# Where the four slots of split weights lie in on-chip memory, in an fp32 three-block network

## What is computed

```python
x = layer_norm(DN_ALPHA * x + y, mix_ln_g[layer], mix_ln_b[layer])
x = layer_norm(DN_ALPHA * x + swiglu(x, ffn_w_gate[layer], ffn_w_up[layer], ffn_w_down[layer]), ...)
...
ff = jnp.square(jax.nn.relu(h2 @ w_ff1 + b_ff1)) @ w_ff2 + b_ff2
```

## Times and profile before

| What | Value |
|---|---|
| median of 3 runs | 3581.85 us (3581.0 to 3584.57) |
| the profiled execution, device time | 3582.25 us |
| its span from first to last instruction | 3580.5 us |
| TensorE busy | 3502.4 us, 98% of the span, 16054 matmuls |
| VectorE busy | 1783.9 us, 50% |
| ScalarE busy | 1235.5 us, 35% |
| GpSimd busy | 527.4 us, 15% |
| mean granted TensorE clock | 0.986 of full speed |

### The profile page before, as it was taken

The page is one execution under the profiler, slowest core; times in us unless marked ns, Lnnn a source line. Parts: engine busy times, 40 slices in busy tenths (PEclk is TensorE's granted clock), DMA queues, the critical chain, the costliest instruction groups (busy, mean ns, idle before and its releaser), DMA issues. The chain is left out here.

```text
span 3580.5 us, 41711 instructions
## 1 busy us (share of the span) xinstructions
PE 3502.4 (98%) x16054; PEld 2830.2 (79%) x16054; DVE 1783.9 (50%) x2319; ACT 1235.5 (35%) x1795; POOL 527.4 (15%) x302
## 2 busy tenths in 40 slices
PE   9999999999999999999999999999999899999998
PEld 7768888888887777767888888888876778888886
DVE  7986423233256666567423233564567674323235
ACT  4444410111144444455321112355454442212133
POOL 0007100000052000013100000353223530000004
PEclk9999999999999999999999999999999999999999
DMA  3102213122122111112213123322231222111112
GB/s 106 38 33 89 95 59 112 47 78 87 47 82 83 48 42 47 41 58 78 89 59 106 52 83 110 95 89 94 97 98 44 77 89 94 47 47 53 47 59 100
DMA packets 77474, 259.12 MB, mean 72 GB/s; under 512 B 10288, under 2 KB 11696, under 8 KB 77360
## 3 DMA queue, kind: packets, MB, share of 16 engines
q1 hardware_dynamic: 77360, 257.59, 22.4%
HBM read 244.45 MB, written 4.72 MB: 70 GB/s over the span
## 5 line engine op out<-in xcount | busy, mean ns | idle before, releaser
L208 PE MATMUL ps<-xh,whi 128*128 128x512 f32 x2712 | 943.0, 394 | 14.8 <-POOL xl L500 8.2
L208 PE MATMUL ps<-xh,wlo 128*128 128x512 f32 x2712 | 935.3, 391 | 0.0
L208 PE MATMUL ps<-xl,whi 128*128 128x512 f32 x2712 | 935.2, 391 | 0.0
L191 DVE TENSOR_TENSOR wlo<-stage,whi 128x1024 fp32r<-128x1024 f32 (+1 forms) x361 | 507.2, 1405 | 475.7 <-ACT whi L184 474.5
L184 ACT ACTIVATE whi<-stage 128x1024 fp32r<-128x1024 f32 (+1 forms) x361 | 378.0, 1047 | 978.4 <-PE ps L208 952.8
L208 PEld LDWEIGHTS ps<-xh,whi 128*128 128x128 f32 x2712 | 511.8, 189 | 130.8 <-DVE wlo L191 8.5
L208 PEld LDWEIGHTS ps<-xh,wlo 128*128 128x128 f32 x2712 | 511.8, 189 | 107.8
L208 PEld LDWEIGHTS ps<-xl,whi 128*128 128x128 f32 x2712 | 511.9, 189 | 105.4
L208 PE MATMUL ps<-hh,whi 128*128 128x512 f32 x1216 | 415.4, 391 | 4.0 <-DVE wlo L191 1.9
L208 PE MATMUL ps<-hh,wlo 128*128 128x512 f32 x1216 | 414.0, 390 | 0.0
L208 PE MATMUL ps<-hl,whi 128*128 128x512 f32 x1216 | 413.8, 390 | 0.0
(11 more groups left out here) (453 smaller groups left out, 4008.7 us busy)
## 6 DMA issues: line engine op xcount, KB each, us to landing
stage<-in_w_ff SPq DMA_DIRECT2D x88, 512.0 KB, 3.5
stage<-in_w_gate SPq DMA_DIRECT2D x59, 512.0 KB, 3.4
stage<-in_w_up SPq DMA_DIRECT2D x59, 512.0 KB, 3.4
stage<-in_w_in SPq DMA_DIRECT2D x50, 512.0 KB, 3.4
ada<-in_w_ada SPq DMA_DIRECT2D x48, 512.0 KB, 3.5
stage<-in_w_qkv SPq DMA_DIRECT2D x43, 512.0 KB, 3.4
stage<-in_w_down SPq DMA_DIRECT2D x48, 448.0 KB, 3.3
stage<-in_w_out SPq DMA_DIRECT2D x24, 512.0 KB, 3.4
```

The costliest lines, as they stand in the source:

```text
L191: dve.tensor_tensor(wlo[slot][:, n], stage[slot][:, n], whi[slot][:, n].bitcast(F32), ALU.subtract).then_inc(w_split, 1)
L208: done = pe.matmul(acc[:, h * HALF:(h + 1) * HALF], wt[slot][:, w], xt[:, b, h * HALF:(h + 1) * HALF], start=b == 0 and wt is whi and xt i ...
```

## The change

Eleven small tiles and `cols` and `ident` are allocated in another order, so that some lie ahead of each slot. The slots are no longer one block: `whi0` starts 192 bytes past a multiple of 512, `whi1` 256, `wlo0` 384 and `wlo1` 448. Each slot is as large as before. `x`, `xh`, `xl`, `stage` and the region with `hh` and `hl` stay at the addresses that they had. `ident` starts 448 bytes past a multiple of 512 and not at one. The instructions of each engine, their order, their shapes and their waits are the same.

```diff
     stage = [sb(f"stage{k}", [P, D]) for k in range(2)]
-    WHI_AT = [nc.sbuf_base + 4 * D * k for k in range(2)]
-    whi = [sb(f"whi{k}", [P, D], F32R) for k in range(2)]
-    WLO_AT = [nc.sbuf_base + 4 * D * k for k in range(2)]
-    wlo = [sb(f"wlo{k}", [P, D], F32R) for k in range(2)]
-    cols = sb("cols", [P, NCOLS])
-    ident = sb("ident", [P, P])
+    stats = sb("stats", [P, 2, 2, 6])
     one = sb("one", [P, 1])
     share = sb("share", [P, 2])
-    stats = sb("stats", [P, 2, 2, 6])
     eps = sb("eps", [P, 1])
+    WHI_AT = [-(-nc.sbuf_base // 32) * 32]
+    whi = [sb("whi0", [P, D], F32R)]
     credit = sb("credit", [P, 9])
-    ps = [ctx.enter_context(nc.psum_tensor(f"ps{k}", [P, S], F32)) for k in range(4)]
+    WHI_AT += [-(-nc.sbuf_base // 32) * 32]
+    whi += [sb("whi1", [P, D], F32R)]
     gb2 = sb("gb2", [P, DB])
     ada_sum = sb("ada_sum", [P, 2])
     lam_t = sb("lam_t", [P, 8])
     mx = sb("mx", [P, 2, 2])
+    WLO_AT = [-(-nc.sbuf_base // 32) * 32]
+    wlo = [sb("wlo0", [P, D], F32R)]
     nb = sb("nb", [P, 2, 2])
     den = sb("den", [P, 2, 2])
+    WLO_AT += [-(-nc.sbuf_base // 32) * 32]
+    wlo += [sb("wlo1", [P, D], F32R)]
+    cols = sb("cols", [P, NCOLS])
+    ident = sb("ident", [P, P])
+    ps = [ctx.enter_context(nc.psum_tensor(f"ps{k}", [P, S], F32)) for k in range(4)]
     rden = sb("rden", [P, 2, 2])
```

## The result

The changed kernel takes 3625.76 us (median of 4 runs, 3624.03 to 3634.66), the kernel before 3581.43 beside it (4 runs, 3580.15 to 3584.57): a ratio of 1.0127 with a 95% interval of 1.011 to 1.0145. The change costs 44 us. The forecast was 81 us less; the time lies inside the range, on the side of the slower rival.

What follows compares the result with a forecast made beforehand. The prediction took TensorE's stream of 512-column matmuls at a 226.7 ns pitch as the bound. Half of 12.7 ns, 6.35 ns x 12,792 = 81 us, came off 3582 to give 3501 us; range 3420 to 3642.

Steps and rivals of the forecast that it cites:

- the slower rival: L208 stretches: with `whi` and `wlo` 192 bytes apart the pitch stays at 231.7 ns; 59 us added, 3641 us; chance 0.28.
- What bounds the kernel: TensorE's stream of 512-column matmuls, 12,792 at a pitch of 226.7 ns, 2,900 us, four fifths of the time.
- I forecast that they do [meet less at a distance]: 512-column matmuls: weight loads and moving operand meet less when their starts differ modulo 512; half of 12.7 ns goes, 81 us.
- The price that I put at -6.35 ns: Expected pitch change per 512-column matmul at L208 and L1349; over 12,792 matmuls, 81 us saved.
- The likeliest case: Fewer meetings in the 512-column stream: 3420 to 3575 us, likeliest 3501; chance 0.44.
- Reads of the next weights in the way of reads of the moving operand: Mechanism claimed for the 12.7 ns by which the 512-column pitch of 226.7 exceeds 214 ns.
- the 12.7 ns: Part of the steady 226.7 ns pitch of 512-column matmuls over 214 ns; all of it gone would save 162 us.
- the bound: Upper limit for L208: the pitch stays for good at its unsettled 231.7 ns, adding 59 us.
- The sign that the two slots would have pitches of their own: Profile after, at L208: if slots count singly, units in slot 0 and slot 1 have two different pitches.
- the settling after a break: Trace before: six pitches after a break average 231.7 ns, the next five 226; taken as two streams meeting in a pattern.
- the rival of no change: 512-column stream: the extra 12.7 ns are paid whatever the addresses, so time stays 3582 us; chance 0.28.
- the 260-column matmuls: At L3050, 120.0 ns each, 11.3 over 108.7; expected to gain or lose about as much each as 512-column ones.

Runs made afterwards that it cites:

- The fourth kernel of set 1: Against the kernel before: both `whi` at multiples of 512 and both `wlo` 192 bytes past one, by moving four small tiles between them; 3621.35 us.

## Why the prediction came out as it did

**What bounds the kernel: right.** The stream of 512-column matmuls sets the time, the pitch is the whole question, and the four measures that I wanted unchanged (counts, order, load length, ScalarE and VectorE) are unchanged. `ident` and `cols` cost nothing that shows: all slots at 256 with both moved came to 3580.87.

**"I forecast that they do [meet less at a distance]": the step that failed.** It rested on two streams that start in the same piece being "the worst pair". The reverse is so: of all settled values 226.67 at distance 0 is the lowest, and none of the 18 kernels of the experiments has a pitch below it in its long piece. The price that I put at -6.35 ns is +4.35. The likeliest case had the wrong sign. It also counted the 1,008 matmuls of L1349 at the same price. In their pieces of six they stand at 231.3 ns before and 232.0 after (starts under 260 ns apart), so they had no settled value to lose; the slower rival left them out, rightly.

**"Reads of the next weights in the way of reads of the moving operand": not borne out.** Loads of half and a quarter of the size made the pitch longer, not shorter (229.9 and 231.5), though those matmuls also had fewer output columns. That the extra over 214 ns depends on the load is shown, since its address relative to the moving operand changes the pitch; that it is the load's reads which cost it isn't. What the 12.7 ns are stays open.

**The slower rival: right in its cause and near in size, wrong in that the stream never settles.** It said that the pitch stays unsettled at 231.7 when high and low part stand at different distances. The fourth kernel of set 1, which changes only that, gives 231.1. But this is a settled value: its pitches repeat with every block of six, between 224 and 236 ns. That a mean of this cycle lies so near the mean of six pitches after a break is luck as far as the runs show. Its 59 us counted 5.0 ns where 4.35 were to come (51 us), and nothing for the half clock's 10. It also left out what a distance costs by itself: by the equal distances alone the changed layout's shares would make (2 x 228.9 + 232.6) / 3 = 230.1 in slot 0 and 227.4 in slot 1, 228.8 on average. So of the 4.35 ns some 2.1 are the distances' own price and some 2.2 that of mixing them, if the two can be added, which no run tests for itself. And the bound would not have held for every layout: at distances of 32 to 224 other than 192, the pitch settles above 231.7, at 232.6 to 234.2. The sign that the two slots would have pitches of their own came true (231.4 and 229.9).

**The earlier trace rows read half right.** I used the settling after a break to say that the meeting of two streams matters, which the distances confirm. The same rows said that an aligned stream settles downward, 231.7 to 226. They had no other distance to compare, but what they had spoke for alignment being the good case, and the forecast went the other way on a picture of memory for which there was no row.

**"Pays at the one way out of memory, whatever the addresses", the rival of no change: fallen.** It is true of addresses that differ by multiples of 256; beside these, only 16 and 240 reached 226.67, and not everywhere. The rule that I weighed with it (the Trainium skill, "SBUF — State Buffer", section "Who interferes with whom": independent ports for moving operand and weight load, TensorE waits on nobody) doesn't account for these traces: the same instructions run at 226.7 or 233.4 ns by where the weights lie. The Trainium skill ("TensorE: Matmul & The Clock Gate", section "Back-to-back issue gap") gives a warm gap that comes to 215.8 ns for 512 columns, and calls it that of an isolated matmul. No layout here came nearer to it than 226.67.

**The earlier trace rows carry less than I put on them.** I expected the 260-column matmuls of the Fourier part to change with the others. The mean of their pitches under 130 ns was 119.7 before and 120.7 after, and lies between 119.5 and 120.7 in every kernel. But they can't tell whether alignment helps them. Their blocks follow each other every 2080 bytes inside `xh` and `xl` and the second half starts 1040 bytes on, so nearly all of them stood at a distance other than 0 in the kernel before too. At half clock the 512-column pitch is 426.2 to 427.2 ns in all kernels. The plain fp32 products at L611 keep 429.7, but neither of their operands lies in a slot, and none moved against the other. So the price of the distance was seen on 512-column fp32r matmuls at full clock, and not at half clock; on other forms it stays open.

**What stays open:** by what path the load and the moving stream touch, why the good distance is 0, why mixed distances cost more than their average, and what picks one of the two ways of settling at 16 and 240.

## What to carry to other kernels

Where TensorE runs long streams of fp32r matmuls of 512 columns, start weights and activations at the same address modulo 256 bytes, high and low parts alike, and protect that with padding, since a few small tiles ahead of a slot cost up to 2% of this kernel. Divide a long piece of the chain by its count before you believe that a busy TensorE is as fast as it was: here the busy share is 98% at 3581 and at 3654 us. And where the trace shows a stream that settles at a low value, ask first what makes it settle, and count a change of that as a risk before counting it as a gain.

## What the hardware showed that was not expected

- **Pitches settle into short cycles.** With all slots at 192, starts repeat as 231.67, 225.86 and 229.14 ns; at 32 and 64 as 235 and 231.5. With high and low part at 0 and 192, the cycle has six pitches, from 224 to 236 ns. Within the traces' resolution the sums are whole multiples of 6.67 ns: 226.67 is 34 of them, 3 x 228.89 is 103, 2 x 233.33 is 70, 6 x 231.11 is 208.
- **The same layout can settle in two ways** (16 and 240: 226.67 in the first two feed-forward parts, 228.7 and 232.9 in the last).
- **A shorter load slows the stream** though it ends earlier: 188 ns long at a pitch of 226.7, 135 ns at 229.9 with 64 columns, and 109 ns at 231.5 with 32. The matmuls behind these loads also have fewer output columns, so it isn't shown that the load alone does it.
- **The low value is fragile.** Of the layouts in the table only those at 0 modulo 256 throughout hold it everywhere.
